# Two transformer blocks on one core: token tiles 0 and 1 of the token-major products are finished first, the attention's products are cut into smaller pieces between column sums, and GpSimd makes ten low parts

## The reference

```python
mod = (silu(c) @ ada_w[l] + ada_b[l])            # shift, scale, gate for mixer and FFN
h = rms_norm(x, mix_pre_g) * (1 + scale_m) + shift_m
q, k, v, x_lru, gate = split(h @ w_in)           # 512, 128, 128, 512, 512
attn = sliding_window_attention(rope(q), rope(k), v, sinks)   # chunks of 64, window 128
lru = rg_lru(causal_dwconv(x_lru), ...) * gelu(gate)
y = concat(rms_norm(attn, g_attn), rms_norm(lru, g_lru)) @ w_out
x = x + gate_m * rms_norm(y, mix_post_g)
h = rms_norm(x, ffn_pre_g) * (1 + scale_f) + shift_f
g, val = split(causal_dwconv(h @ w_up))          # 2 x 3072
x = x + gate_f * rms_norm((gelu(g) * val) @ w_down, ffn_post_g)
```

## Time and profile before

| | us |
|---|---|
| median of 3 runs | 1168.52 |
| lowest, highest run | 1166.82, 1176.54 |
| the profiled execution's own time | 1175.43 |
| its span, first to last instruction | 1173.6 |

### The profile page before, as it was taken

One profiled execution on the slowest core, in us unless ns is written; L12 is line 12 of the kernel. 1 busy time (PEld: TensorE's weight loads), 2 busy tenths in 40 slices (PEclk: granted clock), 3 DMA queues, 4 the chain that ended last, 5 costly groups with the idle time before them and its releaser, 6 DMA issues.

```text
span 1173.6 us, 14312 instructions
## 1 busy us (share of the span) xinstructions
PE 1134.6 (97%) x5672; PEld 952.0 (81%) x5672; DVE 799.7 (68%) x1221; ACT 568.9 (48%) x958; POOL 52.1 (4%) x110
## 2 busy tenths in 40 slices
PE   6999898999999999999999899999999999999997
PEld 6986686988888888888889678888888888888886
DVE  7989957777678777777575595577644565345645
ACT  4488935754224422444377695484432444134441
POOL 3000100000111012000000000000000000000000
PEclk7999888999999999999999898999999999999999
DMA  9853345334775548743322311224223232242321
GB/s 356 333 192 108 92 179 199 106 97 141 248 268 179 167 160 317 180 145 111 105 73 90 71 57 58 76 69 141 90 76 122 90 106 92 72 126 90 105 93 72
DMA packets 49283, 159.88 MB, mean 136 GB/s; under 512 B 9408, under 2 KB 9664, under 8 KB 49216
## 3 DMA queue, kind: packets, MB, share of 16 engines
q1 hardware_dynamic: 33968, 118.57, 31.0%
q0 software_dynamic: 10368, 37.75, 9.4%
q10 hardware_dynamic: 4880, 2.64, 0.9%
HBM read 156.83 MB, written 2.11 MB: 135 GB/s over the span
## 4 chain that ended last, share of the span: by engine, by line
PE 83%; DVE 7%; ACT 5%; DMA 2%; issue 1%; SPq 0%; DVEq 0%; ACTq 0%
PE ps L1772 48%; PE ps L1797 34%; DMA sb_raw<-in_w 2%; DVE sb_wL L1124 1%; ACT sb_wH L593 1%; DVE sb_stage L1130 1%; ACT sb_y L651 1%; ACT sb_y L643 1%; DMA sb_R<-in_ada 1%; DVE sb_x L1202 1%; DVE sb_xc L1410 1%; ACT sb_y L659 0%; DVE sb_hL L1224 0%; ACT sb_hH L666 0%; PE ps L1885 0%
## 5 line engine op out<-in xcount | busy, mean ns | idle before, releaser
L1772 PE MATMUL ps<-sb_hH,sb_wH 128*128 128x512 f32 x832 | 326.3, 392 | 1.3 <-DVE sb_xc L1410 0.8
L1772 PE MATMUL ps<-sb_hL,sb_wH 128*128 128x512 f32 x832 | 324.6, 390 | 0.0
L1772 PE MATMUL ps<-sb_hH,sb_wL 128*128 128x512 f32 x832 | 324.5, 390 | 0.0
L1124 DVE TENSOR_TENSOR sb_wL<-sb_raw,sb_wH 128x1024 fp32r<-128x1024 f32 x182 | 220.9, 1221 | 84.8 <-ACT sb_wH L593 84.4
L593 ACT ACTIVATE sb_wH<-sb_raw 128x1024 fp32r<-128x1024 f32 x182 | 190.1, 1053 | 166.5 <-DMA sb_raw<-in_w 166.2
L1797 PE MATMUL ps<-sb_wH,sb_mH 128*128 128x512 f32 x512 | 204.5, 399 | 1.4 <-ACT sb_adaw L839 1.4
L1797 PE MATMUL ps<-sb_wL,sb_mH 128*128 128x512 f32 x512 | 202.8, 396 | 0.0
L1797 PE MATMUL ps<-sb_wH,sb_mL 128*128 128x512 f32 x512 | 202.1, 395 | 0.0
L1772 PEld LDWEIGHTS ps<-sb_hH,sb_wH 128*128 128x128 f32 x832 | 156.7, 188 | 39.3 <-issue 7.1
L1772 PEld LDWEIGHTS ps<-sb_hH,sb_wL 128*128 128x128 f32 x832 | 156.6, 188 | 32.8
L1772 PEld LDWEIGHTS ps<-sb_hL,sb_wH 128*128 128x128 f32 x832 | 156.7, 188 | 32.2
(11 more groups left out here) (217 smaller groups left out, 1149.6 us busy)
## 6 DMA issues: line engine op xcount, KB each, us to landing
sb_raw<-in_w SPq DMA_DIRECT2D x182, 512.0 KB, 3.5
sb_adaw<-in_ada POOLq DMA_DIRECT2D x42, 512.0 KB, 4.8
sb_stage<-in_ada SPq DMA_DIRECT2D x24, 512.0 KB, 14.2
sb_vw<-in_ada POOLq DMA_DIRECT2D x20, 512.0 KB, 5.0
sb_raw<-in_w SPq DMA_DIRECT2D x8, 384.0 KB, 14.3
sb_stage<-in_ada POOLq DMA_DIRECT2D x6, 512.0 KB, 4.3
sb_x<-in_x SPq DMA_DIRECT2D x4, 512.0 KB, 5.9
sb_x<-in_xt SPq DMA_DIRECT2D x4, 512.0 KB, 6.7
```

The costliest lines, as they stand in the source:

```text
L1124: TT(low_of(n), raw_of(n), high_of(n).bitcast(fp32), ALU.subtract).then_inc(w_lo, 1)
L1772: return nc.tensor.matmul(out, a, b, start=start, stop=stop, **kw)
```

## The change

GpSimd makes the low parts of ten chunks (`POOL_LO`): of both layers O0+6, O0+7, U0 and U0+1, of layer 1 also B+0 and B+1. A new semaphore `w_pool` counts them; `low_done(n)` names the semaphore and value to wait for, and VectorE's `lo_chunk` skips them. In layer 0, GpSimd makes the first two between the fills of units 37 and 38, the next two after that of unit 42, the other six after all fills.

```diff
+        POOL_LO = [l * NCH + c for l in range(DEPTH) for c in
+                   ([0, 1] if l else []) + [NPROJ + 6, NPROJ + 7, NPROJ + NOUT, NPROJ + NOUT + 1]]
+
         def w_no(n):
             return n - GRP + 1
+
+        def low_done(n):
+
+            if n in POOL_LO:
+                return w_pool, POOL_LO.index(n) + 1
+            return w_lo, w_no(n) - sum(1 for m in POOL_LO if m < n)
 
         def pcol(l, name, i=0):
...
+            def lo_chunk(n):
+
+                pool.wait_ge(w_hi, w_no(n))
+                GTT(low_of(n), raw_of(n), high_of(n).bitcast(fp32), ALU.subtract).then_inc(w_pool, 1)
+
             for u in LATE_UNITS[5:]:
                 pool.wait_ge(ada_used, unit_used(u - 5 if u < OUT_UNITS.stop + 3 else u - 3))
                 ada_fill(u)
+                if u == OUT_UNITS.stop - 3:
+                    for n in POOL_LO[0:2]:
+                        lo_chunk(n)
+                if u == OUT_UNITS.stop + 2:
+                    for n in POOL_LO[2:4]:
+                        lo_chunk(n)
+            for n in POOL_LO[4:]:
+                lo_chunk(n)
```

```diff
-                            if h == 0 and (i, kt) == (0, KT - 1):
+                            if h == 0 and (i, kt) == (0, KT - 1 if k else KT // 2 - 1):
                                 transposes(l, k, 2)
-                            if h == 0 and (i, kt) == (1, KT - 1 if k else KT // 2 - 1):
+                            if h == 0 and (i, kt) == (1, KT // 2 - 1 if k else 1):
                                 transposes(l, k, 3)
...
+            def late_tiles(l, stage, k):
+
+                lower, upper = range(KT // 2), range(KT // 2, KT)
                 turning = k == 0 or l + 1 < DEPTH
-                first = KT // 2 if stage == OUT_ else 0
-                for t in (0, 1):
-                    for kt in range(first, KT):
-                        if t == 0 and kt % 2 == 0 and kt >= first:
-                            pe.wait_ge(w_lo, w_no(l * NCH + tm_first(stage) + KP * fh + kt // 2))
-                        token_products(l, stage, fh, t, kt, kt == 0)
-                for t in (2, 3):
-                    if stage == OUT_:
-                        pe.wait_ge(y_read, read_no(l, stage, 0, t - 2))
-                    elif t == 3:
-                        pe.wait_ge(y_read, read_no(l, stage, 0, 0))
-                    for kt in range(KT // 2):
-                        token_products(l, stage, fh, t, kt, kt == 0)
-                for t in (2, 3):
-                    if turning:
-                        transposes(l, k, t - 2)
-                    for kt in range(KT // 2, KT):
-                        token_products(l, stage, fh, t, kt, False)
+                run_of(l, stage, 0, 2, upper)
+                run_of(l, stage, 0, 3, upper)
+                if turning:
+                    transposes(l, k, 0)
+                pe.wait_ge(y_read, read_no(l, stage, 0, 0))
+                run_of(l, stage, 1, 2, lower)
+                if turning:
+                    transposes(l, k, 1)
+                run_of(l, stage, 1, 2, upper)
+                pe.wait_ge(y_read, read_no(l, stage, 0, 1))
+                run_of(l, stage, 1, 3, range(KT))
+
+            def last_down(l, ready):
+
+                lower, upper = range(KT // 2), range(KT // 2, KT)
+                for kt in range(KT):
+                    if kt % 2 == 0:
+                        weights_of(l, DOWN2, 0, kt // 2)
+                    for t in (0, 1):
+                        if kt == 0:
+                            pe.wait_ge(y_read, read_no(l, DOWN1, 1, t))
+                        token_products(l, DOWN2, 0, t, kt, kt == 0, ready if t == 0 else None)
+                pe.wait_ge(f_taps, f_no(l, 2 * PAIRS - 1))
+                for kt in lower:
+                    for t in (2, 3):
+                        token_products(l, DOWN2, 0, t, kt, kt == 0)
+                for kt in lower:
+                    if kt % 2 == 0:
+                        weights_of(l, DOWN2, 1, kt // 2)
+                    for t in (0, 1):
+                        token_products(l, DOWN2, 1, t, kt, kt == 0)
+                weights_of(l, DOWN2, 1, 2)
+                weights_of(l, DOWN2, 1, 3)
+                run_of(l, DOWN2, 1, 0, upper)
+                run_of(l, DOWN2, 1, 1, upper)
+                late_tiles(l, DOWN2, 1)
```

`attn_products` becomes pieces of six products; layer 0's order and its start in layer 1 (whose rest is cut up in the same way):

```diff
+                def attn_products(fh, t, part):
+
+                    if part == 0 and fh == 0:
+                        if t == 0:
+                            pe.wait_ge(gates_done, (l + 1) * LT)
+                        if t == 1:
+                            pe.wait_ge(s_exp, (l + 1) * QT)
+                        tiles = t + 1 if t < 2 else QT
+                        pe.wait_ge(attn_hi, l * QT + tiles)
+                        pe.wait_ge(attn_lo, l * QT + tiles)
+                    if t == 0:
+                        weights_of(l, OUT_, fh, part)
+                    run_of(l, OUT_, fh, t, (2 * part, 2 * part + 1))
...
                     in_tile(13, 1)
+                    attn_products(0, 0, 0)
                     open_cols()
                     attn_cols(0)
                     outputs_mm(2)
-                    attn_products(0, 0)
-                    attn_products(0, 1)
+                    attn_products(0, 0, 1)
+                    attn_products(0, 1, 0)
                     attn_cols(1)
+                    attn_products(0, 1, 1)
+                    attn_cols(2)
                     probs_transposed(3)
-                    attn_cols(2)
+                    attn_products(1, 0, 0)
                     outputs_mm(3)
+                    attn_products(1, 1, 0)
                     lru_cols(0)
                     attn_cols(3)
-                    attn_products(0, 2)
                     lru_cols(1)
+                    attn_products(1, 0, 1)
                     lru_cols(2)
+                    attn_products(1, 1, 1)
                     lru_cols(3, True)
-                    attn_products(0, 3)
+                    attn_products(0, 2, 0)
+                    attn_products(0, 3, 0)
                     norm_spread(1 + l, 7, ratio)
-                    attn_products(1, 0)
-                    attn_products(1, 1)
+                    attn_products(0, 2, 1)
+                    attn_products(0, 3, 1)
...
-                    attn_products(0, 0)
+                    attn_products(0, 0, 0)
                     open_cols()
                     attn_cols(0)
+                    attn_products(0, 0, 1)
                     probs_transposed(3)
-                    attn_products(0, 1)
+                    attn_products(0, 1, 0)
                     attn_cols(1)
+                    attn_products(0, 1, 1)
                     outputs_mm(3)
+                    attn_products(1, 0, 0)
...
                 for kt in range(AT, KT):
-                    token_products(l, OUT_, 0, 3, kt, False)
-                finishing(l, OUT_, 0)
+                    if kt % 2 == 0:
+                        weights_of(l, OUT_, 0, kt // 2)
+                    for t in (0, 1):
+                        token_products(l, OUT_, 0, t, kt, False, lru_ready if t == 0 else None)
+                weights_of(l, OUT_, 1, 2)
+                run_of(l, OUT_, 1, 0, (4, 5))
+                weights_of(l, OUT_, 1, 3)
+                run_of(l, OUT_, 1, 0, (6, 7))
+                run_of(l, OUT_, 1, 1, range(AT, KT))
+                late_tiles(l, OUT_, 0)
```

ScalarE's `tile_chains`, and its order where layer 1's attention opens:

```diff
                 y_square(l, k, 1, 0)
-                split_step(n0)
                 y_root(l, k, 0)
                 y_square(l, k, 1, 1)
                 x_root(l, k, 0)
                 y_root(l, k, 1)
                 x_scaled(l, k, 0)
-                split_step(n0 + 1)
+                y_square(l, k, 0, 2)
                 x_root(l, k, 1)
                 x_scaled(l, k, 1)
+                y_square(l, k, 0, 3)
                 tmp_lower(l, k, 0)
                 hi_part(l, k, 0, 0)
                 hi_part(l, k, 0, 1)
-                y_square(l, k, 1, 2)
                 tmp_lower(l, k, 1)
                 hi_part(l, k, 1, 0)
                 hi_part(l, k, 1, 1)
+                split_step(n0)
+                split_step(n0 + 1)
+                y_square(l, k, 1, 2)
                 y_root(l, k, 2)
+                x_root(l, k, 2)
+                x_scaled(l, k, 2)
+                y_square(l, k, 1, 3)
+                y_root(l, k, 3)
                 split_step(n0 + 2)
-                y_square(l, k, 1, 3)
-                x_root(l, k, 2)
-                y_root(l, k, 3)
                 split_step(n0 + 3)
-                x_scaled(l, k, 2)
                 x_root(l, k, 3)
                 x_scaled(l, k, 3)
-                if k:
-                    split_step(n0 + 4)
                 tmp_lower(l, k, 2)
                 hi_part(l, k, 2, 0)
                 hi_part(l, k, 2, 1)
                 if k:
-                    split_step(n0 + 5)
+                    split_step(n0 + 4)
                 tmp_lower(l, k, 3)
                 hi_part(l, k, 3, 0)
```

(41 more changed lines are left out.)

116 lines of the change are left out of this document (52 added, 64 removed).

## The result

Eleven runs of each kernel: 1181.15 us (1177.46 to 1183.25) with the change, 1172.92 (1166.58 to 1176.54) without, a ratio of 1.0083, 95% interval 1.0063 to 1.0103. The change costs about 10 us (the ratio gives 9.7, the two medians differ by 8.2) where the forecast was a gain of 3. Its profiled execution took 1183.10 us, span 1181.3, which is 7.7 more than the span of before.

What follows compares the result with a forecast made beforehand. TensorE was busy 97% of the span, so only its waits and low-clock time could be won. Terms -1.1 - 6.6 - 2.3 - 6.5 + 3.2 + 3.8 + 7.2 - 0.9 = -3.2 gave 1165 us against the 1168.5 median; range 1150 to 1178.

Steps and rivals of the forecast that it cites:

- the front: Everything ahead of the norms: AdaLN units -1.1, column sums -6.6 and -2.3, opening of layer 1's attention -6.5 us.
- the norms: Three norm stretches, expected to lose: layer 1 after out-projection +3.2, before layer 1's projection +3.8, layer 0 +7.2 us.
- part 2: Column sums: pieces of six products between the sums keep TensorE's clock high, -6.6 us in layer 0, -2.3 in layer 1.
- Rival C: Column sums: six products between sums leave TensorE at 1.2 GHz, -1.4 and 0 instead, 1173 us; chance 0.12.
- Part 3: Opening of layer 1's attention: value copy before the splits removes TensorE's wait and slow matmuls, -6.5 us.
- Part 1: AdaLN units 16 and 17 before chunks 7 and 8 fill VectorE's idle time, -1.1 us.
- Parts 4 to 6: Norms of layer 1 after out-projection, before layer 1's projection, and layer 0: longer waits from engine order, +3.2, +3.8, +7.2 us.
- T1 to T3: In a norm, transposes of token tile 1 to those of tile 3: T3 can start 21.25 us after T1.
- T0 of layer 0: Token tile 0's transposes in layer 0's norm: at S+28.0 us, formerly S+33.4, S being the start of the ratio's spread.
- Rival A: Norms: GpSimd's and VectorE's two-operand subtracts exclude each other, delaying tile 2's update, 6.6 us, 1172; chance 0.28.
- Part 7: Tail: (1,2) ends two runs before (1,3), so VectorE is free when the last tile comes, -0.9 us.
- A with C: Both slower rivals together: GpSimd holds VectorE in the norms, and pieces fail to hold the clock; counted within slower, 0.10.

Runs made afterwards that it cites:

- experiment 4: The kernel before with all of the change ahead of the norms (AdaLN units, pieces between column sums, opening of layer 1's attention): ratio 0.9927.
- experiment 1: The changed kernel with VectorE making all ten low parts that GpSimd made: ratio 1.0057 to the kernel before.
- experiments 3 and 12: On the kernel before: 3 changed only ScalarE's order in the opening of layer 1's attention, 0.9954; 12 only the finer pieces between column sums, 0.9979.
- experiment 14: Experiment 4's kernel with VectorE's order of the last ten AdaLN units as in the change: ratio 0.988, 1154.85 us.
- experiment 8: Experiment 1's kernel with split n0+2 before tile 3's root, tile 3's update before low parts, the projection's last split before tile 3's high parts: 0.9956.
- experiment 9: Experiment 8's kernel with tile 2's square and update also ahead of the first two splits and low parts: ratio 0.993.
- experiment 6: Experiment 1's kernel with each norm's first two splits and low parts back in the gaps of tiles 0 and 1: ratio 1.0233.
- experiment 13: The changed kernel plus 64 probe GpSimd steps of four kinds on an unused buffer in layer 1's feed-forward: ratio 1.0091.
- experiment 2: The kernel before with only GpSimd making the same ten low parts, nothing else of the change: ratio 1.004.

## Why the prediction was wrong

**The sum** was -16.5 for the front, +14.2 for the norms, -0.9 for the tail and nothing for a hold. Measured: front -8.5 (experiment 4), norms +15.2 by order (experiment 1 against 4), GpSimd +3 to +5, tail 0. So of the 13 us between the forecast and the result 8 are the front, mostly part 2, and 3 to 5 are the hold, which the sum put at nothing; the norms and the tail are 1 us each.

**Part 2 failed most: "-6.6" and "-2.3" measure 2.4 together** (0.4 to 4.4). Layer 1's is right by its stretch (-3.0). Layer 0's was sized against one execution, whose stretch was the longest of the three seen without the pieces, 1.6 above their mean; and the pieces were to leave "one stretch at 1.2 GHz, 1.2 us". Against the traces at clock 1.00 that holds in seven executions of thirteen (0 or 1.6 us lost); in six it is 4.8 us or more. Rival C is half right: the pieces do not hold the clock reliably. Why the same sequence now holds it and now does not stays open, and so does why 3.7 and 3.0 by the stretches come down to 2.4 in the times.

**Part 3** was right: -6.5, measured -5.4 alone, -7.4 in the trace. **Part 1** cannot be told from noise: of experiment 4's 8.5 us, experiments 3 and 12 leave 0.7 for it.

**Parts 4 to 6: the mechanism was right,** and the sum of 14.2 meets 15.2, partly by luck: without GpSimd's low parts the three norms are 4.7, 5.2 and 5.5 us longer, where 3.2, 3.8 and 7.2 were worked out with them. It is also a net figure. The earlier AdaLN units give some 5 us back (experiment 14), and against the same units with the norms of before, experiment 1 loses 20.7 us by the times and 19.0 by the norms. Of the order, tile 3's part with the late last split (experiment 8) and the splits ahead of tile 2 (experiment 9) were undone, and both paid. T1 to T3, worked out as 21.25, is 21.93 in the kernel without GpSimd's part. What was missed is the clock: a wait inside the group is followed by slow products. From T3 to the feed-forward that is 1.6 to 2.0 us in the norms of layers 0 and 1, by the traces of experiment 1 and of the change against experiment 8; only 1.0 was put in, for layer 0. And T0 of layer 0 came at S+26.8, 1.2 before the 28.0. The prediction says nothing of why the splits stand behind tile 1; experiment 6 showed what stands behind that, the slots.

**Rival A was right and had 0.28.** It was kept out of the sum because no row showed the hold. Its 6.6 us meet the measured 5 to 7, though steps were held that it did not name, and in the projection's norm not the update. Taken with the forecast it gave 1172, where 1.0083 times the 1168.5 of then is 1178; the rest is the front's. Relieving VectorE was worth nothing: experiment 1 gives it 12 us more work and is faster.

**Part 7** expected 0.9 from the tail; DOWN2 to the end is 50.4 us in both. TensorE's part of it is 44.2 us instead of 43.5, with a wait of 0.44 for the last chunk, whose load is late, and that takes back what the free VectorE gives.

**The range** ended at 1178. A with C, which is nearest to what happened, was named among the chances but left outside: by the prediction's own terms it is 1172 and 7.5, some 1180. And the kernel before itself ran 4 us slower in the eleven runs than in the three.

## What to carry to other kernels

A weight slot is freed by the last tile that uses it. An order that finishes some tiles first brings the refill late, and with it everything that stands in order behind the refilled slot's first reader; look at the loads before judging an order of squares and splits. GpSimd can take over work from VectorE at no cost only while VectorE's next steps have an operand in PSUM, as the taps here; steps with two operands in SBUF are held, however short they are. A loss to the low clock should be sized from several executions.

## What the runs showed of the hardware

A 128x1024 GpSimd subtract takes 2.46 to 2.55 us (experiment 13 and the changed kernel), twice VectorE's 1.22. In experiment 13 a tensor-scalar of that size takes 1.30, a memset 0.95, and a subtract of 128x256 0.81, a third of the full one for a quarter of its elements. The hold reaches the smallest step, 2.33 us for 128x1 (the changed kernel), and can last for two of GpSimd's steps, 6.15 us for 1.22 (experiment 2). In thirteen traces the same TensorE work of layer 0's sums takes 24.5, 26.1, 29.3 or 30.8 us. The first and third of these lie 4.8 us apart, about as far as the changed kernel's fastest and slowest run (5.8); that the one is the reason for the other was not shown.
